# Squares and source tiles added on VectorE ahead of products with ones, in a two-block kernel bound by TensorE

## The reference, cut to what matters

```python
s   = einsum('bhtd,bhsd->bhts', q, k) * w
num = einsum('bhts,bhsv->bhtv', s, v)
den = sum(s, axis=-1)
h   = num / maximum(abs(den), exp(-m))
```

## Time and profile before

| | us |
|---|---|
| median of 3 runs | 2424.12 (2423.99 to 2424.62) |
| the profiled execution, its whole time | 2424.05 |
| its span in the profile | 2422.5 |
| PE busy | 2408.9 (99%) |
| PEld busy | 2078.4 (86%) |
| DVE busy | 1788.2 (74%) |
| ACT busy | 1162.7 (48%) |

### The profile page before, as it was taken

One profiled execution on the slowest core, in us unless ns is written; L12 is line 12 of the kernel. 1 busy time (PEld: TensorE's weight loads), 2 busy tenths in 40 slices (PEclk: granted clock), 3 DMA queues, 4 the chain that ended last, 5 costly groups with the idle time before them and its releaser, 6 DMA issues.

```text
span 2422.5 us, 34993 instructions
## 1 busy us (share of the span) xinstructions
PE 2408.9 (99%) x12802; PEld 2078.4 (86%) x12802; DVE 1788.2 (74%) x2401; ACT 1162.7 (48%) x1350; POOL 125.8 (5%) x234
## 2 busy tenths in 40 slices
PE   9999999999999999999999999999999999999998
PEld 7888888888888888888888888888888888888887
DVE  6788877699899898677756778756777777777644
ACT  6554445444444444444455545455544444444443
POOL 0000000000000000011102000000000000000000
PEclk9999999999999999999999999999999999999999
DMA  9888775688888888899865555665666666668765
GB/s 332 270 261 254 227 242 181 202 269 283 293 269 288 283 272 293 259 312 311 314 200 153 169 166 166 174 199 162 195 190 187 187 190 190 186 187 277 256 197 165
DMA packets 262129, 557.76 MB, mean 230 GB/s; under 512 B 17360, under 2 KB 18432, under 8 KB 261776
## 3 DMA queue, kind: packets, MB, share of 16 engines
q1 hardware_dynamic: 229920, 444.65, 57.8%
q0 software_dynamic: 28704, 105.18, 13.6%
q10 hardware_dynamic: 3408, 6.60, 0.8%
HBM read 552.13 MB, written 4.23 MB: 230 GB/s over the span
## 4 chain that ended last, share of the span: by engine, by line
PE 96%; DVE 2%; ACT 1%; DMA 1%; issue 0%; DVEq 0%; ACTq 0%
PE PS L1912 36%; PE PS L1919 19%; PE PS L1867 12%; PE PS L1868 12%; PE PS L1869 12%; DVE w_lo L1121 1%; PE PS L2215 1%; DMA w_raw<-in_w_in 1%; PE PS L1905 0%; DVE xr L1743 0%; PE PS L1987 0%; PE PS L2006 0%; PE PS L2007 0%; PE PS L2005 0%; PE PS L1973 0%
## 5 line engine op out<-in xcount | busy, mean ns | idle before, releaser
L598 ACT ACTIVATE w_hi<-w_raw 128x1024 fp32r<-128x1024 f32 x832 | 879.8, 1059 | 1063.1 <-PE PS L1869 435.5
L1121 DVE TENSOR_TENSOR w_lo<-w_raw,w_hi 128x1024 fp32r<-128x1024 f32 x832 | 1015.5, 1225 | 485.8 <-ACT w_hi L598 469.2
L1912 PE MATMUL PS<-xs,w_hi 128*128 128x512 f32 x3792 | 912.2, 391 | 0.0
L1912 PEld LDWEIGHTS PS<-xs,w_hi 128*128 128x128 f32 x3792 | 695.4, 188 | 134.4 <-DVE up_rstd L1497 0.4
L1919 PEld LDWEIGHTS PS<-xs,w_lo 128*128 128x128 f32 x3840 | 492.7, 191 | 18.8 <-issue 0.3
L1919 PE MATMUL PS<-xs,w_lo 128*128 128x256 f32 x3840 | 500.6, 283 | 0.0
L1867 PE MATMUL PS<-w_hi,hs 128*128 128x512 f32 x704 | 274.2, 389 | 0.0
L1869 PE MATMUL PS<-w_hi,hs 128*128 128x512 f32 x704 | 273.9, 389 | 0.0
L1868 PE MATMUL PS<-w_lo,hs 128*128 128x512 f32 x704 | 273.9, 389 | 0.0
L1101 DVE SCALAR_TENSOR_TENSOR mod_w<-mod_w,c_row 128x1024 f32<-128x1024 f32 x192 | 234.1, 1219 | 12.7 <-DMA mod_w<-in_w_mod_rows 11.8
L1867 PE MATMUL PS<-w_hi,xs 128*128 128x512 f32 x564 | 221.5, 393 | 1.3 <-DVE w_lo L1121 1.3
(11 more groups left out here) (307 smaller groups left out, 1376.3 us busy)
## 6 DMA issues: line engine op xcount, KB each, us to landing
w_raw<-in_w_up SPq DMA_DIRECT2D x352, 512.0 KB, 4.5
w_raw<-in_w_in SPq DMA_DIRECT2D x208, 512.0 KB, 4.4
mod_w<-in_w_mod_rows POOLq DMA_DIRECT2D x192, 512.0 KB, 6.3
w_raw<-in_w_down SPq DMA_DIRECT2D x176, 512.0 KB, 4.9
w_raw<-in_w_out SPq DMA_DIRECT2D x64, 512.0 KB, 4.3
w_raw<-in_w_ple_gate SPq DMA_DIRECT2D x32, 512.0 KB, 4.6
w_raw<-in_w_ple_proj SPq DMA_DIRECT2D x4, 512.0 KB, 6.9
mix<-in_x_cols SPq DMA_DIRECT2D x4, 512.0 KB, 9.2
```

The source lines that it names most:

```text
L598: nc.scalar.activation(w_hi[:, slot, :, :], w_raw[:, slot, :, :], ACT.Copy).then_inc(hi_made, 1)
L1121: V.tensor_tensor(w_lo[:, slot, :, :], w_raw[:, slot, :, :], w_hi[:, slot, :, :].bitcast(F32), ALU.subtract).then_inc(lo_made, 1)
L1912: ins = M(PS[:, bank + b, :], w_hi[:, slot, k, b * P:(b + 1) * P], x(cs[k]), start=begin and k == 0, stop=end and k == GK - 1)
```

## The change

VectorE adds the two squared channel tiles of a head, and TensorE makes one product with ones of the sum, for mLSTM heads 0 to 2 and all GLA heads. For the denominator VectorE adds the two source tiles of the second target tile into a fourth tile beside the three of `m_sw`, and TensorE makes one product of 256 columns whose moving operand is tiles 0 and 3. The semaphore that lets TensorE start its sums now comes after this addition. Head 3's sum of squares stays as it was.

```diff
+    m_by_tile = act_out[:, 2:4, :].rearrange("p a b -> p (a b)").rearrange("p (c n) -> p c n", n=P)
 ...
 (VectorE, mixers1)
+                if n in MLSTM_NORM and j == 0:
+                    wait("m_sq")
+                    V.tensor_tensor(m_sq[:, 0, :], m_sq[:, 0, :], m_sq[:, 1, :], ALU.add).then_inc(S["m_sq_added"], 1)
                 if n in MLSTM_NORM and j == 2:
                     mlstm_var(ps)
 ...
                     if j == 2:
                         wait("m_scores")
                         wait("m_exp")
-                        V.scalar_tensor_tensor(m_sw, PS[:, ps, 0:3 * P], MD ** -0.5, m_w, ALU.mult, ALU.mult)\
+                        steps.do(V.scalar_tensor_tensor(m_sw, PS[:, ps, 0:3 * P], MD ** -0.5, m_w, ALU.mult, ALU.mult))
+                        V.tensor_tensor(m_by_tile[:, 3, :], m_by_tile[:, 1, :], m_by_tile[:, 2, :], ALU.add)\
                             .then_inc(S["m_weighed"], 1)
 ...
 (VectorE, mixers2)
+                if n in GLA_HEAD and j == 6:
+                    wait("g_sq")
+                    V.tensor_tensor(g_sq[:, 0, :], g_sq[:, 0, :], g_sq[:, 1, :], ALU.add).then_inc(S["g_sq_added"], 1)
 ...
 (TensorE)
-                causal_sum(PS[:, ps + 3, 0:T], ones[:, :], ones[:, :], m_sw).then_inc(S["m_num"], 1)
-
-            def mlstm_sum_squares(ps):
-                wait("m_sq")
-                for v in range(2):
-                    ins = M(PS[:, ps + 3, 0:T], ones[:, :], m_sq[:, v, :], start=(v == 0), stop=(v == 1))
+                M(PS[:, ps + 3, 0:T].rearrange("p (c n) -> p c n", n=P), ones[:, :], m_by_tile[:, 0:4:3, :], start=True, stop=True)\
+                    .then_inc(S["m_num"], 1)
+
+            def mlstm_sum_squares(ps, last=False):
+                if last:
+                    pe.wait_ge(S["m_sq"], MH)
+                    for v in range(2):
+                        ins = M(PS[:, ps + 3, 0:T], ones[:, :], m_sq[:, v, :], start=(v == 0), stop=(v == 1))
+                else:
+                    wait("m_sq_added")
+                    ins = M(PS[:, ps + 3, 0:T], ones[:, :], m_sq[:, 0, :], start=True, stop=True)
                 ins.then_inc(S["m_ss"], 1)
 ...
                 if n in GLA_NORM and j == 1:
-                    wait("g_sq")
-                    for v in range(2):
-                        ins = M(PS[:, ps + 3, 0:T], ones[:, :], g_sq[:, v, :], start=(v == 0), stop=(v == 1))
-                    ins.then_inc(S["g_ss"], 1)
+                    wait("g_sq_added")
+                    M(PS[:, ps + 3, 0:T], ones[:, :], g_sq[:, 0, :], start=True, stop=True).then_inc(S["g_ss"], 1)
```

More of the change, by code:

```diff
@@ L364, in two_block_kernel @@
         gate_hi gate_lo gate_ps gate_half gate_sum gate_ln gates_ready y_hi
-        m_scores m_arg m_masked m_exp m_weighed m_num m_floor m_h m_sq m_ss m_var m_std m_og m_y
+        m_sq_added g_sq_added m_scores m_arg m_masked m_exp m_weighed m_num m_floor m_h m_sq m_ss m_var m_std m_og m_y
         f_sq f_var f_std f_scaled f_cols f_queries f_normed cols_turned cols_made
@@ L2133, in mixers1 @@
                 if (n, j) == (11, layers["in1b"].G - 1):
-                    mlstm_sum_squares(ps)
+                    mlstm_sum_squares(ps, last=True)
             def mixers1_end(n, j):
```

## The result

The changed kernel takes 2430.1 us (median of 14 executions, 2427.1 to 2432.0), against 2424.4 before (2423.9 to 2425.0): a ratio of 1.0022, 95% interval 1.0015 to 1.0029. It is slower by 5.7 us.

The account below looks back on a forecast made before the run. TensorE's matmul stream, busy for 99% of the span, was taken to bound the kernel. Savings of 4.0 us and stalls of 7.3 us gave +3.3 on 2424.05, or 2427.4 us, with a range of 2425.2 to 2430.4.

Parts of the forecast that it names:

- What TensorE saves: Seven sums of squares, 3.0 us, and four denominators, 1.0 us: 4.0 us together, bounds 3.0 to 4.4.
- The strided operand: Denominator's moving operand, read in two pieces of 128 columns, 384 apart: taken to cost no change.
- Where additions are covered: Denominator source tiles and GLA squares: VectorE's additions finish before TensorE needs them and cost nothing.
- The three waits: TensorE's sums of squares in strips 8, 9 and 11 wait for VectorE's addition: 2.1, 3.1 and 2.1 us, together 7.3.
- start-ups: After each of the three waits TensorE's second product starts late, losing 0.1 us more.
- the first rival: TensorE's clock falls in the new stalls: 2429.6 us with one fall, 2434 with three; chance 0.14 for at least one.
- slower by over 0.2%: Outcome for the whole kernel, above 2429.0 us, by a clock fall or somewhat longer stalls: chance 0.16.
- two gaps beyond what the trace has seen: Argument for a clock fall: stalls of about 2, 2.9 and 2 us against an earlier longest idle of 1.4.
- the price of one: One clock fall and climb costs about 2.2 us, from slow products at the kernel's start against late ones.
- The second rival: No stall at the mLSTM sums of squares, the addition is there in time: 2420.1 us, chance 0.05.
- The fourth: Rival: stalls partly hidden by later TensorE waits; 2426 us with half of one covered, range 2424 to 2426, chance 0.05.
- The third: Rival: the denominator's strided operand costs as much as three products, 1.0 us of saving missing: 2428.4 us, chance 0.08.

Follow-up runs that it names:

- experiment 3: Changed kernel, with VectorE adding the mLSTM squares two groups earlier, after group 6 of the previous strip, ahead of the evacuation: 2420.0 us, ratio 0.9982.
- experiment 2: Changed kernel without its part on the mLSTM squares; denominators and GLA squares stay changed: 2421.2 us, ratio 0.9988.
- lower bunch: The six executions of the changed kernel's first 14 at 2427.1 to 2428.0 us, listed with a mean granted clock of 0.999.
- experiment 7: Changed kernel with the addition of mLSTM squares one place earlier in VectorE's order, ahead of the split of group 0: 2423.8 us, ratio 0.9999.
- experiment 8: Changed kernel with the addition of mLSTM squares one place later, behind the split of group 1: 2436.5 us, ratio 1.0052.
- second sitting: The later timing session, in which the changed kernel ran again unaltered: 2430.8 us over 8 executions, ratio 1.0027.
- experiment 6: Changed kernel with the early addition for strip 9 only, strips 8 and 11 left in the changed place: 2426.0 us, ratio 1.0006.
- experiment 1: The changed kernel once more, unaltered, profiled in an execution where the clock falls: 2430.8 us, ratio 1.0027.
- upper bunch: The changed kernel's slower executions, 2429.3 to 2432.0 us over both sittings, listed with a mean granted clock of 0.998 or 0.997.
- experiment 5: Changed kernel with the early addition for strips 8 and 11, only strip 9 left in the changed place: 2423.8 us, ratio 0.9998.
- experiment 4: Changed kernel with unused TensorE products (8 in strips 8 and 11, 12 in strip 9) ahead of the wait: 2427.0 us, ratio 1.0011.

## Why the prediction was right, and where it wasn't

**What TensorE saves**, 4.0 us worked out from spacings: right, 4.3 us in experiment 3, of which 3.1 (worked out: 2.7) in experiment 2. The strided operand, taken at no cost between bounds far apart, costs nothing (0.42 us).

**Where additions are covered**: right at all eight places, the four GLA squares and the four denominators. No wait for these additions appeared and experiment 2 kept the full gain.

**The three waits**: right in place, order and size. The list was to show 2, 3 and 2 us less 0.16 and shows 1.92, 2.85 and 1.91. Priced at 7.3 us with their start-ups, they cost 7.5 (lower bunch against experiment 3), or 7.0 by the kernel with its waits filled. The addition takes 0.42 us, as taken from the earlier trace rows. Experiments 7 and 8 moved it by one place either way and the waits followed by 1.1 us each.

**The forecast of 2427.4** is thus the time of the executions in which the clock holds (2427.1 to 2428.0), and of the kernel with the waits filled (2427.0). But it isn't the median. The median of 2430.1 belongs to what stood as the first rival, at 2429.6 with one fall, and the range reached it because of that rival. That it did is in part luck: its end, 2430.4, is 0.3 us away, and the median of the second sitting, 2430.8, lies beyond it. The measured ratio of 1.0022 (1.0015 to 1.0029) also leans to "slower by over 0.2%", which had 0.16.

The step that failed is the chance given to the fall of the clock, 0.14: going by times and listed clocks, at least one fall came in 8 of 14 executions and then in 8 of 8. I had argued against it from the earlier trace rows, that all three idles are shorter than the 4.2 us between the last product and the fall at the end of the trace. That row tells how late one fall came after one stop. It doesn't tell how short a stop is enough, and I used it as if it did; likewise I let the rival decide at strip 9 alone, for having the longest idle, and experiment 6 has the 1.9 us idles bring falls in nine or ten executions of eleven.

The prediction also counts "two gaps beyond what the trace has seen"; by its own figures, against the 1.4 us of the earlier trace rows, there were three. The other term, the price of one, was taken from the slow products at the start at 2.2 us and is 1.6 for the falls of experiment 1. Those products are slow, but the clock column of the kernel before doesn't put it down to the clock, being at 1.00 there:

```profile
0.00:5.00 5.00, 3.35 (x15) 3.35 (x16) 0.00 (x0) 1.49 (x2) 1.69 (x11) 1.00 0.48 147
```

With two falls at the price measured the rival gives 2427.4 + 3.2 = 2430.6, within the upper bunch.

The advice in the Trainium skill, "TensorE: Matmul & The Clock Gate", "Why this matters for your kernels", is to leave no long gaps between bursts of matmuls, and what it warns of came with this change. But the gap from which on it warns is about that of strip 9 and well beyond the 1.9 us of strips 8 and 11, so by its figure these two should have done nothing. The measurement decides: with idles of 1.9 us amid a full stream the clock fell in most executions (experiment 6), and nothing of it shows in the kernels whose longest idle is 1.7 us (experiment 7) or 1.4 us (before).

**The second rival**, no stall at all, is false for the change as it stands and true for the addition two groups earlier, at 2420.0 where it was put at 2420.1. The fourth, a stall partly hidden, isn't seen: the two later waits on norms kept their 2.7 us together. The third, a strided operand that costs as much as three products, is refuted by its 0.42 us.

The mechanism of the loss is shown, and so is that of the two bunches. Left open are why the first sitting had six executions in 14 without a fall and the second none in eight, what decides within one program whether the clock falls, and the one execution at 2426.7 of experiment 5.

## What to carry to other kernels

Where one engine is busy for 99% of the span, an operation moved off it pays only if its result is there before that engine gets to it: look up the place in the other engine's order, not its share of busy time. An addition of 0.42 us cost 2 to 3 us at one place and nothing two groups earlier, because of what stood in front of it. And count a new wait of TensorE of some 2 us at more than its length; if it can't be avoided, products that nobody uses, a little shorter than the wait, cost nothing here and kept the clock up (experiment 4).

## What the hardware showed that I hadn't expected

The granted clock fell to 1.2 GHz after idles of only 1.9 us, in some executions and not in others of the same program, and it did so after work had begun again: in experiment 1 the wait of strip 9 ended at 303.60, the spacing doubled at about 305.0 and was back by 308.5. In experiment 8, with idles of 3.0 and 4.0 us, it fell before the product that ended the wait had begun, by 0.9 us at strip 9 (from 306.36, by the 0.68 of the stretch 306 to 307, to 307.27). A profile taken of a single execution can miss this altogether, as the first one here did, while the mean granted clock listed with each execution (0.999 against 0.998 or 0.997) told the two bunches apart. It is a rough sign, though: the profiled execution of experiment 6 had one fall and is listed with 0.999, like those without any, so a single fall can vanish in its last digit.
